# Four instruction-order moves in a fused transformer layer: turning back the sparse heads, one gate pair, one block of the second down projection

## What is computed

```python
x = x + 0.5 * rms_norm(swiglu(rms_norm(x, g1), w1_gu, w1_down), g1_post)
h = rms_norm(x, gm)
(q_n, kc, vc, ksl, vsl, kwn, vwn, g_n, q_d, k_d, v_d, g_a, g_b) = split(h @ w_in)
y_nsa = nsa_attention(...)       # 8 heads in 2 groups: compressed, selected, window branch
y_dil = dilated_attention(...)   # 12 heads, three dilations, joined by softmax weights
merged = sigmoid(g_a) * (y_nsa @ w_branch_nsa) + sigmoid(g_b) * (y_dil @ w_branch_dil)
x = x + rms_norm(merged @ w_out, gm_post)
x = x + 0.5 * rms_norm(swiglu(rms_norm(x, g2), w2_gu, w2_down), g2_post)
```

## Time and profile before

| | |
|---|---|
| time, median of 3 runs | 1146.07 us (1146.03 to 1146.32) |
| the profiled execution's own time | 1146.04 us |
| its span | 1144.2 us |
| PE busy | 1130.2 us, 99% of the span |
| DVE busy | 790.0 us, 69% |
| ACT busy | 551.6 us, 48% |
| POOL busy | 112.1 us, 10% |
| chain that ended last | PE 96%, DVE 2%, ACT 1%, issue 1% |

### The profile page before, as it was taken

The page is one execution under the profiler, slowest core; times in us unless marked ns, Lnnn a source line. Parts: engine busy times, 40 slices in busy tenths (PEclk is TensorE's granted clock), DMA queues, the critical chain, the costliest instruction groups (busy, mean ns, idle before and its releaser), DMA issues.

```text
span 1144.2 us, 18877 instructions
## 1 busy us (share of the span) xinstructions
PE 1130.2 (99%) x7148; PEld 990.4 (87%) x7148; DVE 790.0 (69%) x1208; ACT 551.6 (48%) x1008; POOL 112.1 (10%) x222
## 2 busy tenths in 40 slices
PE   9999999999999999999999999999999999999997
PEld 7889999988887888887977888887889999998886
DVE  5888888855356365444878553698689888878863
ACT  6245555542225312245778422357445555556543
POOL 0000000056006030000001400002000000000002
PEclk9999999999999999999999999999999999999999
DMA  7313333365954697454200223344233333335541
GB/s 222 108 53 98 110 110 110 111 255 202 377 221 155 205 335 225 129 167 146 78 2 3 76 75 109 121 162 141 74 87 97 95 92 108 110 124 201 204 153 73
DMA packets 148430, 157.99 MB, mean 138 GB/s; under 512 B 4868, under 2 KB 125868, under 8 KB 146812
## 3 DMA queue, kind: packets, MB, share of 16 engines
q1 hardware_dynamic: 139184, 117.46, 33.2%
q0 software_dynamic: 9072, 39.66, 9.7%
q10 hardware_dynamic: 112, 0.03, 0.0%
HBM read 140.10 MB, written 21.49 MB: 141 GB/s over the span
## 4 chain that ended last, share of the span: by engine, by line
PE 96%; DVE 2%; ACT 1%; issue 1%; DVEq 0%; POOL 0%; ACTq 0%; POOLq 0%
PE ps L2188 28%; PE ps L2295 28%; PE ps L2328 10%; PE ps L2354 6%; PE ps L2483 4%; PE ps L2801 3%; PE ps L2373 3%; PE ps L2779 2%; PE ps L2614 1%; PE ps L2638 1%; PE ps L2767 1%; PE ps L2545 1%; PE ps L2584 1%; PE ps L2566 1%; PE ps L2555 1%
## 5 line engine op out<-in xcount | busy, mean ns | idle before, releaser
L1437 DVE TENSOR_TENSOR ring_lo<-ring_raw,ring_hi 128x2048 fp32r<-128x2048 f32 (+1 forms) x56 | 126.3, 2256 | 114.1 <-ACT ring_hi L937 114.1
L937 ACT ACTIVATE ring_hi<-ring_raw 128x2048 fp32r<-128x2048 f32 (+1 forms) x56 | 105.3, 1882 | 188.3 <-PE ps L2328 71.0
L2188 PE MATMUL ps<-xn_hi,ring_hi 128*128 128x512 f32 x472 | 186.1, 394 | 2.7 <-DVE xn_lo L1476 2.3
L2188 PE MATMUL ps<-xn_hi,ring_lo 128*128 128x512 f32 x472 | 183.9, 390 | 0.0
L2188 PE MATMUL ps<-xn_lo,ring_hi 128*128 128x512 f32 x472 | 183.7, 389 | 0.0
L2295 PE MATMUL ps<-s_hi,ring_hi 128*128 128x256 f32 x512 | 144.9, 283 | 0.0
L2295 PE MATMUL ps<-s_lo,ring_hi 128*128 128x256 f32 x512 | 144.9, 283 | 0.0
L2295 PE MATMUL ps<-s_hi,ring_lo 128*128 128x256 f32 x512 | 144.9, 283 | 0.0
L2295 PE MATMUL ps<-x_hi,ring_lo 128*128 128x256 f32 x384 | 108.7, 283 | 0.0
L2295 PE MATMUL ps<-x_lo,ring_hi 128*128 128x256 f32 x384 | 108.7, 283 | 0.0
L2295 PE MATMUL ps<-x_hi,ring_hi 128*128 128x256 f32 x384 | 108.7, 283 | 0.0
(11 more groups left out here) (389 smaller groups left out, 2386.0 us busy)
## 6 DMA issues: line engine op xcount, KB each, us to landing
ring_raw<-in_ffn_w_gu SPq DMA_DIRECT2D x86, 512.0 KB, 4.9
ring_raw<-in_w_in SPq DMA_DIRECT2D x42, 512.0 KB, 4.7
ring_raw<-in_ffn_w_down SPq DMA_DIRECT2D x40, 512.0 KB, 4.3
ring_raw<-weight_sums SPq DMA_DIRECT2D x24, 512.0 KB, 4.0
down_block<-in_ffn_w_down POOLq DMA_DIRECT2D x8, 1024.0 KB, 9.5
weight_sums<-down_block POOLq DMA_DIRECT2D x8, 1024.0 KB, 9.2
out_block<-in_w_out POOLq DMA_DIRECT2D x4, 1024.0 KB, 8.7
weight_sums<-out_block POOLq DMA_DIRECT2D x4, 1024.0 KB, 10.5
```

What stands on the lines that cost most here:

```text
L937: e = act.activation(dst, src, ACT.Copy)
L1437: e = dve.tensor_tensor(dst, src, f32(r), ALU.subtract)
L2188: e = pe.matmul(ps[:, 2 * (slot if pair is None else pair) + c, :], part(a, slot, k * 256 + c * P, P), xn[b][:, k, :], start=(k == 0 and i ...
```

## The change

Six edits, which belong to three places:

- Sparse loop, PE: each `turn_back` moves from the end of a round to just behind `transposes_halved` of the next round.
- Sparse loop, DVE: `take_branch` moves behind the biases of its round.
- Gate steps, DVE: `scale_gate(3)` moves behind the first two takes of the dilated tiles.
- Second feed-forward only: `hi_part(1)` moves into the last up step, ahead of its second silu, and `lo_part(1)` behind the sum for the 12 corner, ahead of the product with the silu.

```diff
@@ down_mixed (ACT)
-                    hi_part(1)
                     for n in range(1, 17):
...
-                mixed(MIXED // 2 - 1, 1, ahead=1, extra={"z": lambda: hi_down(0), "silu": lambda: hi_down(1)})
+                mixed(MIXED // 2 - 1, 1, ahead=1, extra={"z": lambda: hi_down(0), "silu": lambda: hi_down(1), "seed": lambda: hi_part(1) if f else None})
@@ down_mixed (DVE)
-                    lo_part(1)
                     first = {1: lambda: sum_h(1, 0), 2: lambda: sum_h(1, 1), 3: lambda: sum_h(2, 0), 4: lambda: sum_h(2, 1),
...
                     dve.tensor_tensor(h_f32[:, v, 0:256], z, t_part[:, :], ALU.add).then_inc(c12_taken, 1)
+                    also("c12")
...
-                mixed(MIXED // 2 - 1, 1, ahead=1)
+                mixed(MIXED // 2 - 1, 1, ahead=1, extra={"c12": lambda: lo_part(1) if f else None})
@@ sparse loop (DVE)
-                for b, done in ((0, S_DONE), (1, W_DONE)):
-                    j, rest = divmod(pair - done - 4, 5)
-                    if rest == 0 and 0 <= j < HPG:
-                        take_branch(j, b)
                 if P0 < pair <= NP:
                     take_low_pT(pair - 1)
                 for u in (2 * pair + 2, 2 * pair + 3):
...
                         add_bias(u)
+                for b, done in ((0, S_DONE), (1, W_DONE)):
+                    j, rest = divmod(pair - done - 4, 5)
+                    if rest == 0 and 0 <= j < HPG:
+                        take_branch(j, b)
@@ gates (DVE)
-                if i:
+                if i not in (0, 3):
                     scale_gate(i)
...
                         for g in range(3):
+                            if (c, g) == (0, 2):
+                                scale_gate(3)
                             dve.wait_ge(ydT_done, 3 * c + g + 1)
@@ sparse loop (PE)
                 transposes_halved(pair - 1)
+                for b, done in ((0, S_DONE), (1, W_DONE)):
+                    j, rest = divmod(pair - done - 4, 5)
+                    if rest == 0 and 0 <= j < HPG - 1:
+                        turn_back(j, b)
                 if pair + 1 < NP:
                     scores(2 * pair + 2)
...
-                for b, done in ((0, S_DONE), (1, W_DONE)):
-                    j, rest = divmod(pair - done - 3, 5)
-                    if rest == 0 and 0 <= j < HPG - 1:
-                        turn_back(j, b)
```

## The result

| | before | changed |
|---|---|---|
| median | 1146.44 us (1145.41 to 1149.78, 18 runs) | 1148.52 us (1147.62 to 1150.1, 18 runs) |
| profiled execution's span | 1144.2 us | 1145.8 us |

The ratio is 1.0016, with a 95% interval of 1.0010 to 1.0023: by this ratio 1.8 us slower, between 1.1 and 2.6 (the two medians lie 2.1 apart). The forecast was +1.84 us (1147.9 against 1146.07); the median came out at 1148.5, since the kernel before also has a median 0.4 us higher over 18 runs than over its first three. The change is slower clear of noise, and by less than the 0.2% that the prediction had named as its line between "no change" and "slower".

The account below looks back on a forecast made before the run. PE, busy 99% of the span, was taken as the bound. Sparse loop +3.4, gate steps -0.76 and down projection -0.8 gave +1.84 us on 1146.04, so 1147.9 us; range 1145.0 to 1149.6.

Parts of the forecast that it names:

- The bias behind the two moves: Sparse loop, first period: DVE's bias starts at 596.23 instead of 596.33, 0.1 us gained, all that moving `take_branch` gains.
- T behind `take_oT`: Sparse loop: the 16 transposes wait for ACT's copy queued behind `take_oT`, turn back still to come; next scores +0.58 us.
- The place of the turn back: Sparse loop, PE: 0.12 us more per turn back at a change of tile height, six times, 0.7 us in sum.
- V behind the scaling, window branch: Sparse loop: value products wait 0.3 us for bias plus branch scaling, and 1.0 us in the third period's last round.
- V behind the scaling, selected branch: Sparse loop, first period: scaling ends at 598.8, value products' own time 598.54; hidden behind the transposes' wait.
- The later periods: Sparse loop: second period costs 0.9 us, 0.3 more for transposes waiting on ACT's copy; third 1.9; first 0.6.
- The loop that breaks even: Sparse loop: old turn back waits (0.31 x 3) are given back for the new ones; 1144.5 us; chance 0.18.
- the gains given back elsewhere: Gate steps and down projection: 0.76 and 0.8 lost to next `yd` add or third weight block; 1149.4 us; chance 0.10.
- the aim met: All 1.8 us of sparse-loop stalls go and both other gains come; 1142.7 us; chance 0.07.
- Rival 2: Sparse loop: PE's wait for `o_nsa_read`; branch 0.2 us later costs 1.2 more over six places, 1149.1 us; chance 0.15.
- The line of 0.2%: Whole kernel: a measurement can tell about 0.2% (2.3 us) from no change; below 1143.8 faster, above 1148.4 slower.
- rival 3: Outside the loop: gate and down gains given back at new waits, loop as forecast +3.4; 1149.4 us; chance 0.10.

Follow-up runs that it names:

- after_swap: Changed kernel, but ACT copies the head's output after the turned probabilities instead of ahead of them; ratio 1.0008 against the kernel before.
- between_swap: Changed kernel, but ACT copies the turned probabilities ahead of the head's output and DVE scales the branch between copy and biases; ratio 0.9992 against the kernel before.
- last_early: Changed kernel, but the last of the six branch scalings stays ahead of the copy and the biases; ratio 1.0006 against the kernel before.
- loop_only: Kernel before with only the sparse loop's edits (turn back and branch scaling moved); ratio 1.0029 against the kernel before.
- gate_down: Kernel before with only the gate and down projection edits, sparse loop as before; ratio 0.9988 against the kernel before.
- gate_only: Kernel before with only the fourth gate pair's scaling moved; ratio 0.9997 against the kernel before.
- down_only: Kernel before with only the second down block's high and low parts moved; ratio 0.9994 against the kernel before.
- turn_only: Kernel before with only PE's turn back moved in the sparse loop, branch scaling in its old place; ratio 1.0044 against the kernel before.
- branch_only: Kernel before with only DVE's branch scaling moved behind the biases, turn back in its old place; ratio 1.0011 against the kernel before.
- gd_swap: Kernel before with the gate and down edits, and ACT copying the turned probabilities ahead of the head's output; ratio 1.0003 against the kernel before.

## Why the prediction was right, point by point

- **The sum.** Forecast +3.4, -0.76 and -0.8, so +1.84; the traces have +3.36, -0.80 and -0.85, the runs +1.8 (1.1 to 2.6). The mechanisms came as forecast, but that the totals agree within 0.1 us is partly luck: the parts below are off by up to 0.2 us, in both directions.
- **The bias behind the two moves.** "0.1 us, since the scores it was late for are late themselves": 0.10 measured. The sentence calls this all that moving the scaling gains, and that holds only for the bias and only beside a late turn back: against the turn back's move alone the scaling's move saves the loop some 1.7 us (5.1 against 3.4).
- **T behind `take_oT`.** T was put 600.2 - 593.99 = 6.2 us after its fellow two rounds ahead; it came 599.99 - 593.75 = 6.24 after. `after_swap` shows the cause.
- **The place of the turn back.** 0.64 against 0.52, in the trace at each turn back, and 0.13 to 0.15 over the three steps T, B, S in `between_swap`. The forecast had 0.12 or 0.13 each, 0.7 in all; measured are 0.85. The prediction weighed a rule of the Trainium skill ("TensorE: Matmul & The Clock Gate", "Step-by-step: what each phase is for") by which the 0.12 would vanish. That rule asks for one of two conditions, and the first does not hold here: a weight load for all 128 rows has row groups in common with the transposes still running on 64 of them. Only the second, a load into the background buffer, could have hidden it; the rows show that something is exposed, and no run shows whether it is the load. That the change of tile height is the reason is read from which neighbours cost 0.64 and which 0.52, not from an experiment.
- **V behind the scaling, window branch.** Forecast 0.3 and, in the last round, 1.0; measured 0.28 by the row and 1.10, and `last_early` took 1.11 back.
- **V behind the scaling, selected branch.** The step failed in its detail: I had it hidden behind T's wait. V does wait there (0.27 by the row), and T's wait behind it is shorter by as much. The sum did not change, since both hang on the same two engines in the same round.
- **The later periods.** Forecast 0.6, 0.9, 1.9; measured 0.70, 0.82, 1.84. The term that was off is T's wait at each later period's first turn back: put at 0.3, measured 608.77 - 607.62 - 1.03 = 0.12. The two sides of this wait each moved by about 0.1 us. ACT's copy was early: the bias came at 605.41 (the forecast's 605.7 is 605.46 in this trace, which runs 0.24 ahead), and the exponentials began 0.73 us after it, at 606.14, instead of 0.8. And PE itself was late, since the first period had cost 0.1 more than forecast.
- **Rivals.** The loop that breaks even fell with `loop_only`; the gains given back elsewhere fell with `gate_down`, `gate_only` and `down_only`; the aim met fell with the row of waits. Rival 2, that all six waits for `o_tmp` show, was half true: all six show, 0.27 or 0.28 each and 1.02 the last, but not on top of T's wait.
- **The line of 0.2%.** The forecast put the change within it with 0.50 and beyond it with 0.43; the ratio's interval reaches across it. (The range's upper end, 1149.6, is 0.2 above the 1149.4 of rival 3 that it is said to end at; nothing hangs on it.)

## What to carry to other kernels

Moving an instruction out of a wait pays only if what now comes first is ready: here the turn back waited 0.3 us, but it had filled the time in which the transposes would have waited for a copy that is issued after the turn back's own. Before moving work on one of several engines that are all near 90% busy, walk one full period with all of them and look for two things: who releases a buffer that the next but one step needs, and what stands ahead of the releasing instruction in its own queue. And when a change has several parts, time the parts: two here were worth 1.6 us and a third took twice that away, and the one number of the whole shows neither.

## What the hardware showed that I had not expected

**The granted clock fell once in the loop, behind rounds with long waits.** In the profiled execution of `turn_only` the last round's value products took 637.32 - 635.41 = 1.91 us instead of 1.02. The windows of that stretch (eighth column PEclk; the first had waits in it, the others are dense):

```profile
632.00:636.00 4.00, 3.21 (x38) 2.57 (x40) 2.33 (x9) 2.54 (x7) 0.60 (x1) 0.83 0.00 0
636.00:638.00 2.00, 2.00 (x26) 1.67 (x24) 1.23 (x8) 1.42 (x7) 0.68 (x1) 0.50 0.00 0
638.00:642.00 4.00, 4.00 (x38) 3.20 (x34) 1.73 (x2) 3.41 (x6) 0.00 (x0) 1.00 0.01 4
```

After a loop whose rounds had waits of 1.3 us, the granted clock was at its 1.2 GHz level for some 3 us. The groups from 634.4 to 638.2 show what it cost: S took 0.33 us more than in the rounds before, V 0.89 and T 0.28, 1.5 in all. The first two periods of the same loop had the same waits and a clock of 1.00, and no other profiled execution showed a fall in the loop. It need not be rare in this kernel: of its five runs one has a mean granted clock of 1.000 and took 1150.6 us, the other four have 0.998 and took 1151.4 to 1152.4. Where in the program those lost their clock no run shows.

**It also fell where nothing was changed.** The first up step of the second feed-forward, just behind the layer's second renewal of `x`, in `gate_down` and then in the kernel before:

```profile
800.00:803.00 3.00, 3.00 (x11) 2.32 (x10) 2.19 (x2) 2.06 (x2) 0.00 (x0) 0.59 0.00 0
```

```profile
800.00:803.00 3.00, 3.00 (x17) 2.42 (x16) 2.19 (x4) 2.75 (x3) 0.00 (x0) 1.00 0.00 0
```

PE did 11 matmuls there against 17. The stretch from the dilated tiles to the down products was so 1.6 us longer in that execution (351.15 against 349.54), which hides the two gains in its span: 1144.1 against 1144.2. `down_only` had it too (0.69 over 798 to 803), the profiled executions of the other kernels, before and changed among them, had 1.00 here. `branch_only` and `gd_swap` had a fall at the other such place, behind the layer's first renewal of `x` (0.76 and 0.61 over 363 to 366, where before had 1.00). The kernel before had the same idle time ahead of this place (PE busy 2.66 of 4 us over 796 to 800, against 2.72 in `gate_down`) and kept its clock; what decides was not tried. One execution's span is thus no measure of an effect of 1 us; the lengths of the groups at the place of the edit are.
